# Block 1's queries and top keys before tile 1's output projection, the memory projection in five parts, and one more gather slot up to expert 59

## What is computed

```python
def peer_ffn(xn, w_pq, sub_keys, u_tab, v_tab):      # per block of 128 tokens
    q = (xt @ w_pq).reshape(128, 8, 2, 128)
    s = einsum('thcd,hckd->thck', q, sub_keys)
    s1, i1 = top_k(s[:, :, 0], 16); s2, i2 = top_k(s[:, :, 1], 16)
    top, sel = top_k(all sums s1 + s2, 16)            # 16 experts per token and head
    gate = softmax(top)
    h = einsum('td,thkd->thk', xt, u_tab[idx])        # 16384 experts, rows of 1024 floats
    return einsum('thk,thkd->td', gelu(h) * gate, v_tab[idx])

x = x + token_mixer(rms_norm(x)) @ w_out   # sliding window attention beside a gated MLP
x = x + memory_attention(rms_norm(x))      # 256 memory tokens, keys and values projected here
x = x + peer_ffn(rms_norm(x))              # all experts' rows are gathered from HBM
y = rms_norm(x)
```

## Time and profile before

| | us |
|---|---|
| median of 3 runs | 1723.54 |
| lowest and highest run | 1721.8, 1724.96 |
| profiled execution | 1718.98 |
| its span, first to last instruction | 1717.2 |
| PE, DVE, ACT, POOL busy | 1305.9, 1172.2, 811.7, 660.5 |
| moved by DMA | 656.30 MB, 604.28 MB of it gathers |

### The profile page before, as it was taken

How to read it: one execution, slowest core, us unless ns; L and a number is a source line. 1 busy time by engine, 2 the same in 40 slices (tenths; PEclk the granted TensorE clock), 3 DMA queues, 4 the chain that set the end, 5 groups by cost and what they waited for, 6 DMA issues and landing times.

```text
span 1717.2 us, 21560 instructions
## 1 busy us (share of the span) xinstructions
PE 1305.9 (76%) x7059; PEld 472.4 (28%) x7059; DVE 1172.2 (68%) x2762; ACT 811.7 (47%) x2338; POOL 660.5 (38%) x583
## 2 busy tenths in 40 slices
PE   7999877797888776667877767776776776677765
PEld 3454522342443321223322211211211111111110
DVE  2444567888676777677777777777666677677764
ACT  1433455776344455455555454455444445444443
POOL 0000134334444434344444554434444444444441
PEclk9999988798999988989898887778888878877866
DMA  9434699999999999999999999999999999999995
GB/s 361 157 109 150 251 348 384 379 398 378 421 422 420 419 406 420 401 408 417 421 421 421 421 421 421 421 422 421 421 421 421 421 404 422 422 421 421 420 421 235
DMA packets 97890, 656.30 MB, mean 382 GB/s; under 512 B 12449, under 2 KB 17185, under 8 KB 20961
## 3 DMA queue, kind: packets, MB, share of 16 engines
q0 software_dynamic: 83056, 604.28, 85.5%
q1 hardware_dynamic: 14720, 50.64, 7.8%
HBM read 651.66 MB, written 4.19 MB: 382 GB/s over the span
## 4 chain that ended last, share of the span: by engine, by line
DMA 45%; PE 25%; DVE 11%; ACT 10%; issue 7%; POOL 1%; ACTq 0%; DVEq 0%; SPq 0%; POOLq 0%
DMA R<-in_peer_uv,R 45%; PE ps L1967 9%; PE ps L1512 6%; DVE R L1436 4%; PE ps L1489 3%; ACT L892 2%; PE ps L1771 2%; ACT R L901 2%; ACT R L896 2%; ACT R L892 1%; PE ps L1497 1%; DVE R L1266 1%; DVE R L1267 1%; DVE R L1269 1%; POOL R L621 1%
## 5 line engine op out<-in xcount | busy, mean ns | idle before, releaser
L1967 PE MATMUL ps<-R 64*64 64x512 f32 x4608 | 752.8, 735 | 381.1 <-ACT R L901 375.2
L621 POOL DMA_INDIRECT R<-in_peer_uv,R x576 | 658.5, 1143 | 961.8 <-PE ps L1967 763.6
L1436 DVE CUSTOM_DVE_ANT_0 R<-R 128x1024 f32<-128x1024 f32 x576 | 700.1, 1225 | 381.5 <-DMA R<-in_peer_uv,R 372.0
L892 ACT ACTIVATE R<-R 128x1 f32<-128x1 f32 x576 | 115.8, 201 | 600.3 <-DVE R L1436 591.9
L1967 PEld LDWEIGHTS ps<-R 64*64 64x64 f32 x4608 | 138.2, 150 | 736.8 <-ACT R L901 632.0
L901 ACT ACTIVATE R<-R 128x64 f32<-128x64 f32 x576 | 200.4, 348 | 53.2 <-ACT R L896 0.4
L1771 PE MATMUL ps<-A,R 128*128 128x256 f32 (+1 forms) x640 | 223.6, 474 | 0.7 <-ACT R L782 0.7
L896 ACT ACTIVATE R<-R 128x1 f32<-128x1 f32 x576 | 169.8, 295 | 20.9
L1771 PEld LDWEIGHTS ps<-A,R 128*128 128x128 f32 (+1 forms) x640 | 94.5, 199 | 262.7 <-issue 260.2
L1512 PE MATMUL ps<-A,R 128*128 128x512 f32 (+1 forms) x256 | 100.4, 544 | 0.0
L1489 PE MATMUL ps<-R 128*128 128x256 f32 (+2 forms) x384 | 92.2, 394 | 0.0
(11 more groups left out here) (280 smaller groups left out, 881.2 us busy)
## 6 DMA issues: line engine op xcount, KB each, us to landing
R<-in_peer_uv,R POOLq DMA_INDIRECT x576
A<-in_w_pq SPq DMA_DIRECT2D x8, 1024.0 KB, 10.2
A<-in_w_in SPq DMA_DIRECT2D x3, 2048.0 KB, 22.2
R<-in_w_out SPq DMA_DIRECT2D x5, 1024.0 KB
R<-in_w_out SPq DMA_DIRECT2D x1, 3072.0 KB
R<-in_w_mkv SPq DMA_DIRECT2D x2, 1024.0 KB, 9.3
R<-in_x_promptT SPq DMA_DIRECT2D x4, 512.0 KB, 8.6
x_res<-in_x_prompt SPq DMA_DIRECT2D x4, 512.0 KB, 11.4
```

What stands on the lines that cost most here:

```text
L621: pool.indirect_dma_start(slots[slot_of[g]], None, I["peer_uv"][:, :], bass.IndirectOffsetOnAxis(ap=idx[:, b % 4, k:k + 1], axis=0)).then_ ...
L892: act.activation(hgelu[:, b % 2, col], hdot[:, b % 2, col], ACT.Gelu).then_inc(gelu_ready, 1)
L1436: dve.tensor_tensor_reduce(u, u, xn(t), 1.0, 0.0, ALU.mult, ALU.add, hdot[:, b % 2, k:k + 1]).then_inc(u_used, 1)
L1967: ins = pe.matmul(bank(2 * (t % 2) + q)[rows], diag[tokens, g % DIAGS, :], v_rows[slot_of[g]][tokens, c * 512:(c + 1) * 512], start=first, ...
```

## The change

- The memory projection's inputs come in five parts (chunks 0, 1, 2-3, 4-5, 6-7), ten loads instead of four; PE takes chunk after chunk, both column blocks within it. Ahead of it POOL zeroes 384 columns of `R` and PE multiplies them five times into bank 7.
- A slot 9 is laid over the residual rows of tiles 3 and 4 in `x_res`. Phases become six slots from step 0, seven from 16, eight from 34, seven from 60. Step 59 is the last in slot 9; after it SP loads the rows of tiles 3 and 4 again (1 MB), ahead of the four loads of `w_out`'s pieces, and `out_add` of tiles 3 and 4 waits for them.
- PE runs block 1's query product before tile 1's output projection, its transposition and its scores within it. ACT and DVE take block 1's queries, scores and top keys ahead of step 0. DVE adds tile 1's projection after step 1.
- Tile 1's steps move: its memory steps 3 later, the norm before its experts 2 later, and the units and output pieces of tiles 2 to 4 2 later.

```diff
-SLOT_PHASES = ((0, (0, 1, 2, 3, 4)), (13, (0, 1, 2, 3, 4, 5)), (31, (0, 1, 2, 3, 4, 5, 7)),
-               (140, (0, 1, 2, 3, 4, 5)), (225, (0, 1, 2, 3, 4, 5, 6)), (278, tuple(range(9))))
+SLOT_PHASES = ((0, (0, 9, 1, 2, 3, 4)), (16, (0, 9, 1, 2, 3, 4, 5)), (34, (0, 1, 2, 3, 4, 5, 7, 9)),
+               (60, (0, 1, 2, 3, 4, 5, 7)), (140, (0, 1, 2, 3, 4, 5)), (225, (0, 1, 2, 3, 4, 5, 6)), (278, tuple(range(9))))
+MKV_PARTS = ((0, 1), (1, 2), (2, 4), (4, 6), (6, 8))
...
+        slots.append(x_res[:, 3 * D:5 * D])
...
-        PREP_AT = {1: -1, 2: 122, 3: 200, 4: 210}
-        QUERY_AT = {1: 5, 2: 134, 3: 208, 4: 218}
-        CROSS_AT = {1: 8, 2: 138, 3: 222, 4: 244}
-        FFN_AT = {1: 28, 2: 158, 3: 268, 4: 16 * 23 + 2}
-        UNIT_AT = (22, 29, 36, 43, 50, 57)
-        OUT_AT = (75, 79, 83, 89, 93, 97, 103, 107, 111, 117, 121, 125)
+        PREP_AT = {1: 2, 2: 122, 3: 200, 4: 210}
+        QUERY_AT = {1: 8, 2: 134, 3: 208, 4: 218}
+        CROSS_AT = {1: 11, 2: 138, 3: 222, 4: 244}
+        FFN_AT = {1: 30, 2: 158, 3: 268, 4: 16 * 23 + 2}
+        UNIT_AT = (24, 31, 38, 45, 52, 59)
+        OUT_AT = (77, 81, 85, 91, 95, 99, 105, 109, 113, 119, 123, 127)
...
-            for i in range(2):
-                k = slice(4 * i, 4 * i + 4)
-                load(mem_T[:, k], v3(I["memT"][:, :], KD)[:, k], ld_memT[i])
-                load(w_mkv[:, k], v3(I["w_mkv"][:, :], KD)[:, k], ld_wmkv[i])
+            for i, (a, b) in enumerate(MKV_PARTS):
+                k = slice(a, b)
+                load(mem_T[:, k], v3(I["memT"][:, :], KD)[:, k], ld_mkv[i])
+                load(w_mkv[:, k], v3(I["w_mkv"][:, :], KD)[:, k], ld_mkv[i])
...
+            sp.wait_ge(v_used, max(g for g in range(BLOCKS * TOPK) if slot_of[g] == 9) + 1)
+            for t in range(3, TILES):
+                load(xr(t), I["x_prompt"][0, (t - 1) * P:t * P, :], ld_x[t])
...
+            pool.memset(R[:, 8192:8576], 0.0).then_inc(warm, 1)
...
-                    elif g == 1:
+                    elif slot_of[g] in (1, 2):
                         pool.wait_ge(wo_done, 2)
-                    elif g == 3:
+                    elif slot_of[g] in (3, 4):
                         pool.wait_ge(wo_done, 3)
+                    elif slot_of[g] == 9:
+                        pool.wait_ge(x_std, TILES)
...
             act.activation(mv_l, mv, ACT.Copy).then_inc(mv_moved, 1)
+            queries_out(1)
             gates(0, 0)
+            queriesT_out(1)
+            scores_out(1)
...
             act.wait_ge(sgu_out, TILES)
-            prep(1, 0)
-            queries_out(1)
-            queriesT_out(1)
-            scores_out(1)
...
             finish_gates(0, 0)
-            dve.wait_ge(wo_done, 3)
-            dve.tensor_tensor(xr(1), xr(1), ps[:, 1024:2048], ALU.add).then_inc(x1_out, 1)
+            for c in range(2):
+                top_keys(1, c)
...
+                    if g == 1:
+                        add_one()
...
+                if n < 3 and t > 2:
+                    dve.wait_ge(ld_x[t], 48)
...
-            for j in range(2):
-                for k in range(KD):
...
+            pe.wait_ge(warm, 1)
+            for _ in range(5):
+                pe.matmul(bank(7)[:, 0:384], R[:, 8192:8320], R[:, 8192:8576], start=True, stop=True)
+            for k in range(KD):
...
             scores(0)
+            q_mm(1)
             pe.wait_ge(n_T, 1)
             pe.wait_ge(h_T, 4)
-            for c in range(2):
-                product(bank(2 + c), lambda k: T1[:, k, :], lambda k: w_out[:, 2 * c:2 * c + 2, k, :]).then_inc(wo_done, 1)
-            q_mm(1)
...
+            out_one(0, 0, 2)
             q_T(1)
+            out_one(0, 2, 4)
             scores(1)
+            out_one(0, 4, KD)
+            out_one(1, 0, KD)
```

More of the change, by code:

```diff
@@ L312, in hybrid_step @@
         ld_tab, ld_mem, ld_small = (sem(n) for n in ("ld_tab", "ld_mem", "ld_small"))
-        ld_wmkv = [sem(f"ld_wmkv{i}") for i in range(2)]
+        warm = sem("warm")
+        ld_mkv = [sem(f"ld_mkv{i}") for i in range(len(MKV_PARTS))]
         ld_gains = sem("ld_gains")
-        ld_memT = [sem(f"ld_memT{i}") for i in range(2)]
         ld_x = [sem(f"ld_x{t}") for t in range(TILES)]
@@ L605, in _ @@
                         pool.wait_ge(v_used, held_by(g) + 1)
-                    elif g == 0:
+                    elif slot_of[g] == 0:
                         pool.wait_ge(h_tr, TILES - 1)
                         pool.wait_ge(stored, 16 * 4)
-                    elif g == 1:
+                    elif slot_of[g] in (1, 2):
                         pool.wait_ge(wo_done, 2)
-                    elif g == 3:
+                    elif slot_of[g] in (3, 4):
                         pool.wait_ge(wo_done, 3)
+                    elif slot_of[g] == 9:
+                        pool.wait_ge(x_std, TILES)
                     elif slot_of[g] == 5:
@@ L984, in _ @@
             dve.wait_ge(ld_gains, 16)
[L985 to L988, removed]
+            for i, (a, b) in enumerate(MKV_PARTS):
+                part = mem_T[:, a:b]
+                dve.wait_ge(ld_mkv[i], 32)
+                dve.tensor_tensor(part, part, gains_of(G_MEM, a, b, NMEM), ALU.mult).then_inc(mg_ready, 1)
             def rope(src, dst, t, n):
@@ L1319, in _, with add_one @@
             finish_gates(0, 0)
-            dve.wait_ge(wo_done, 3)
-            dve.tensor_tensor(xr(1), xr(1), ps[:, 1024:2048], ALU.add).then_inc(x1_out, 1)
+            for c in range(2):
+                top_keys(1, c)
+            def add_one():
+                dve.wait_ge(wo_done, 3)
+                dve.tensor_tensor(xr(1), xr(1), ps[:, 1024:2048], ALU.add).then_inc(x1_out, 1)
             def prep_rows(t):
@@ L1437, in _ @@
                     for n, step in query_steps(g):
-                        if n == 1 and step in (16, 17):
-                            top_keys(1, step - 16)
                         if n > 1 and step in (14, 15):
@@ L1490, in product @@
                 return ins
-            for j in range(2):
-                for k in range(KD):
-                    if j == 0 and k % 4 == 0:
-                        pe.wait_ge(ld_wmkv[k // 4], 16)
-                        pe.wait_ge(mg_ready, k // 4 + 1)
+            pe.wait_ge(warm, 1)
+            for _ in range(5):
+                pe.matmul(bank(7)[:, 0:384], R[:, 8192:8320], R[:, 8192:8576], start=True, stop=True)
+            for k in range(KD):
+                for i, (a, _) in enumerate(MKV_PARTS):
+                    if k == a:
+                        pe.wait_ge(ld_mkv[i], 32)
+                        pe.wait_ge(mg_ready, i + 1)
+                for j in range(2):
                     ins = pe.matmul(bank(4 + j), mem_T[:, k, j * P:(j + 1) * P], w_mkv[:, k, :], start=(k == 0),
                                     stop=(k == KD - 1))
-                ins.then_inc(mkv_done, 1)
+                    if k == KD - 1:
+                        ins.then_inc(mkv_done, 1)
             def project(t, c, first=0, end=KD):
@@ L1810, in _, with out_one @@
             scores(0)
+            q_mm(1)
             pe.wait_ge(n_T, 1)
             pe.wait_ge(h_T, 4)
-            for c in range(2):
-                product(bank(2 + c), lambda k: T1[:, k, :], lambda k: w_out[:, 2 * c:2 * c + 2, k, :]).then_inc(wo_done, 1)
-            q_mm(1)
+            def out_one(c, first, end):
+                for k in range(first, end):
+                    ins = pe.matmul(bank(2 + c), T1[:, k, :], w_out[:, 2 * c:2 * c + 2, k, :], start=(k == 0),
+                                    stop=(k == KD - 1))
+                if end == KD:
+                    ins.then_inc(wo_done, 1)
+            out_one(0, 0, 2)
             q_T(1)
+            out_one(0, 2, 4)
             scores(1)
+            out_one(0, 4, KD)
+            out_one(1, 0, KD)
             def prep(t, step):
```

## The result

The changed kernel takes 1725.70 us (median of 22 runs, 1723.05 to 1731.5) where the kernel before, on the same chips, takes 1723.52 (22 runs). The ratio is 1.0015, 95% interval [1.0009, 1.0022]: slower by 0.15%, which is 2.6 us, inside the 0.2% that was called no change, where 13 us of gain were forecast. The profiled execution took 1723.05 us with a span of 1721.3, against 1717.2 before.

The account below looks back on a forecast made before the run. It took PE to bound the start and full DMA the time from 410 us, with neither full from 208.5 to 410. 4.0 + 5.5 + 4.5 - 1.0 = 13.0 us off 1723.5 gave 1710.5 us, range 1702 to 1719.

Parts of the forecast that it names:

- Part 5: Tile 1's steps and later units moved 2 or 3 steps later: same instructions, nobody late, so no cost.
- Part 1: Memory projection at the start: PE begins earlier on smaller input parts; 4.0 us gained, bounds 1.5 and 5.3.
- the bound: At the start: memory rows reach ACT at 40.1 whatever PE does, leaving 1.3 us; gains over 5.3 us are lost.
- loads landing "as before": At the start: x and w_in land as before despite six more issues, since bytes ahead are equal and DMA is full.
- own figure for small parts: At the start: small loads at 301 GB/s would bring x and mem_prompt rows 3 us later, leaving 2.2 us gain.
- Part 2: New order at 196 us: gathers go earlier and close most of the DMA loss up to 245; 5.5 us gained.
- Part 3: One more slot, steps 16 to 59: earlier gathers win 4.5 of 12.1 us lost from 245 to 388; bounds 0, 9.
- Part 4: Reload of 1.05 MB around the hole before step 64: costs 1.0 us, between 0 and 2.5.
- The engines set the pace: Up to step 67 DVE, ACT and PE wait for each other, the slot gains nothing: 6.5 us gained, 1717.0; chance 0.16.
- The clock rival: PE clock near 0.6 from 340 to 410 us: 17 us more, 1727.5; chance 0.10 shared with other gain-eating waits.

## Why the prediction was wrong

Forecast 1710.5, measured 1725.70: outside the range. The step that failed is **Part 5, the moved steps, which ends in "Nothing"**. It looked at who wants each moved result, and at PE's weights, and found nobody late; that holds, no wait of the moved query product for its weights is in the trace. It did not ask what stands beside each moved step on its engine. Two pieces of work that were two steps apart came to lie on each other: block 3's gates ahead of the copy of tile 1's expert input, and unit 3's exponentials and transposition ahead of block 4's scores. The moved steps cost 10.9 us by themselves and 11.7 us on top of the other parts. These are within 1 us of each other, so no interaction with the slot or the order shows.

The second place shows how. These rows are of the changed kernel:

```profile
352.71 1.28 ACT L879 ACT_TABLE_LOAD   x1
...
356.19 1.28 ACT L899 ACT_TABLE_LOAD   x1
...
358.51 1.09 PE L1997 MATMUL ps<-R 64*64 64x512 f32 x8 [3.19 <-ACT R L908]
...
360.25 1.91 PE L1959 MATMUL ps<-ident,R 128*128 128x128 f32 x8
...
363.67 0.71 PE L1811 MATMUL ps<-R 128*128 128x128 f32 x4
```

ACT works from 352.71 to 357.5 on unit 3's exponentials and two table loads. PE waits 3.19 us for the expert behind them, then transposes unit 3, and only then makes block 4's scores, at 363.67; before the change the transposition came two steps ahead of the scores, now it is in the same step. VectorE stands from 359 to 364.84, and the experts and slots behind it wait too. That this chain, and not one piece of it, is the cause at the second place is argued from these rows and from the run with block 4's queries one step earlier; no run takes out unit 3's table loads alone, and that run's profile shows only part of its loss.

The other parts, against their own terms:

- **Part 1: 4.0 forecast.** PE's marks at 8.23 and 22.04 came within 0.4 us. What was mis-sized is the bound: it held the memory rows at 40.1 "whatever PE does", and they came at 41.88; their load was issued at 17.60 instead of 16.52 and took 24.3 us instead of 23.5. The 1.3 us of slack were gone: PE waited 0.28 us for bank 2 here and 1.0 with the start alone. 3.4 us were left at 46.54, 2.8 at the first gather, and 1.6 [-0.2, 3.3] in the time of the start alone. The bound named the right place and the wrong number; the sentence on loads landing "as before" was the mistake. So was its ground, that the DMA is full from the start: from 2 to 6 us it moved 184 GB/s, before 256. The prediction's own figure for small parts, 2.2 us, is nearer to the 1.6 than the 4.0 that it took.
- **Part 2: 5.5 forecast, no gain that shows.** The mechanism came true in the full change (409 GB/s up to 245 us), and its time did not. Alone the order gives -1.2 us [-3.3, 1.0], on top of start and slot 1.6 us (0.9947 against 0.9956, intervals overlapping). But in both of these versions tile 1's addition stands ahead of step 0, and they have 319 and 351 GB/s up to 245 us: by these rows the rate came with the late addition, and that came with the moved steps. In the version with steps one less, which has the order in full, VectorE is 10.9 us ahead at step 50 and 9.6 at step 56; with start and slot alone it is 7.5 and 8.7 ahead. So 3.4 us of lead become 0.9 at the wait for block 4's scores. No run has the late addition with unmoved steps.
- **Part 3: 4.5 less the reload's 1.0.** Measured, with the reload in both, 4.1 alone and 5.3 when taken away. Right.
- **Part 4: 1.0, bounds 0 and 2.5.** Without the reload the time was 1.0023 of before instead of 1.0015, the intervals overlapping: no price that can be measured, so the lower bound.
- **The rivals.** "The engines set the pace" has the right kind of cause, waits of DVE, ACT and PE for each other, and forecast 1717.0, because it took them as they were and not as the moved steps would make them. The clock rival is out: in the windows from 290 on PE was granted 0.75 to 0.87, not 0.6, and where it was lowest PE had waited for ACT. The Trainium skill (TensorE: Matmul & The Clock Gate, Part 1) ties the clock to how busy PE has been, and the trace agrees: 0.95 with 30.90 of 36.5 us busy, 0.75 with 34.31 of 50. Row by row the tie is loose: 15.02 of 22, the same share, had 0.84. That the low clock follows the waits and doesn't make them is argued from this; no run holds the clock.
- **The range** took its lower bounds from the terms of gain, and gave all waits that could eat it 0.10. For all parts but Part 5 9.1 us [6.9, 11.4] were measured, not 13.0: that time would have been inside the range, with Parts 1 and 2 too large and the reload too dear.

Two things stay open: the second place, where the chain is argued, and the 7.2 us of one step in block 4's queries, of which the profiles show the smaller part. The start and the slot together (7.6 us) give a little more than one by one (5.7); the intervals allow for both.

## What to carry to other kernels

When a hand-written order is shifted by a few steps, draw up for each engine what stands in the steps that it now meets, and not only who needs the shifted result: here a copy of 0.58 us behind two table loads, and scores behind a unit's exponentials and transposition, cost more than three real improvements won. Count a lead where the same work has been done on both sides: a moved piece makes it look larger just ahead of its new place. Undo the "free" part of a change first when its sum doesn't come out; here that one run was 11.7 us faster than the whole change. A lead won early counted here only as far as the next wait whose time was set by something else.

## What the runs showed of the hardware

- Splitting 3.1 MB of loads in ten pieces of 128 to 512 KB, where there had been two pairs of 512 KB and 1 MB, went with a lower rate in the first microseconds and with the same rate later:

```profile
2.00:6.00 4.00, 0.00 (x0) 0.00 (x0) 0.13 (x1) 0.00 (x0) 0.57 (x1) 1.00 0.93 256
2.00:6.00 4.00, 4.00 (x9) 2.26 (x8) 0.00 (x0) 0.00 (x0) 0.59 (x2) 1.00 0.86 184
```

The first row is of the kernel before, the second of the changed one. With the start alone the row has 199. From 6 to 10 us the two kernels have 350 and 351 GB/s, from 10 to 14 us 443 and 434. 72 GB/s less for 4 us are 0.29 MB, about 0.7 us at 421 GB/s. The memory rows, issued behind, reached ACT 1.8 us later. The Trainium skill (DMA: Bandwidth & Descriptors, section Bandwidth) asks for at least 1 MiB for each DMA, and up to 6 us the trace agrees; behind that no loss shows. PE began earlier all the same.

- The first products of PE were slow again while the row of 1 to 7 us says a granted clock of 1.00: ten of 384 columns took 5.29 us, 0.53 each on average, where 0.33 would be full rate by 0.438 for 512 columns. The real ones behind them took 13.97 us for 32, 0.437 each, full rate.
- A load of the activation table took 1.28 us wherever it stood, and moving the gates of one block by two steps, so that a pair of such loads no longer stood ahead of the copy, brought the ratio from 1.0015 to 0.9997.
- 1.05 MB of loads beside gathers, at a time when slots and not bytes were short, cost nothing that could be measured: 1.0023 of before without them, 1.0015 with them.
